# Gate and up weights of three expert groups moved as one whole expert per transfer, with each expert's columns dealt to four column groups of TensorE

## The reference, cut to what matters

```python
def expert_choice_moe(x, w_router, b_router, w_gate, w_up, w_down):
    cap = CAPACITY_FACTOR * s // N_EXPERTS                      # 2 * 256 // 16 = 32 tokens an expert
    aff = softmax(x @ w_router + b_router)                      # 16 experts
    gate, idx = lax.top_k(aff.transpose(0, 2, 1), cap)
    xs = x[bidx, idx]                                           # (16, 32, 1024)
    hid = silu(einsum('becd,edf->becf', xs, w_gate)) * einsum('becd,edf->becf', xs, w_up)
    ys = einsum('becf,efd->becd', hid, w_down) * gate[..., None]
    return zeros_like(x).at[bidx, idx].add(ys)
```

## Time and profile before

| What | Value |
|---|---|
| Time, median of 3 runs | 1989.81 us (1985.96 to 1994.66) |
| Profiled execution, its own time | 1984.02 us |
| Its span, first to last instruction | 1982.2 us |
| Mean granted TensorE clock | 0.970 |
| PE, DVE, ACT busy | 1744.1, 697.8, 298.5 us |
| Data moved | 599.64 MB, mean 303 GB/s |

### The profile page before, as it was taken

How to read it: one execution, slowest core, us unless ns; L and a number is a source line. 1 busy time by engine, 2 the same in 40 slices (tenths; PEclk the granted TensorE clock), 3 DMA queues, 4 the chain that set the end, 5 groups by cost and what they waited for, 6 DMA issues and landing times.

```text
span 1982.2 us, 20644 instructions
## 1 busy us (share of the span) xinstructions
PE 1744.1 (88%) x8516; PEld 904.6 (46%) x8516; DVE 697.8 (35%) x1456; ACT 298.5 (15%) x805; POOL 121.2 (6%) x105
## 2 busy tenths in 40 slices
PE   6999999999999999998878787777998878787776
PEld 3466988544679974474222122212474222122211
DVE  1673556977528986273010010101273010010101
ACT  1142000011611001252000010001253000010000
POOL 0000000000013510310000000000210000000000
PEclk9999999999999999999999899999999999999999
DMA  9890888755225643546999999999646999999997
GB/s 346 328 337 23 276 281 298 281 203 182 86 85 185 241 152 130 173 170 255 397 425 428 426 428 425 428 429 405 188 170 244 381 425 428 425 428 426 428 428 303
DMA packets 166925, 599.64 MB, mean 303 GB/s; under 512 B 18752, under 2 KB 77760, under 8 KB 135104
## 3 DMA queue, kind: packets, MB, share of 16 engines
q1 hardware_dynamic: 166606, 598.03, 76.9%
q10 hardware_dynamic: 242, 0.53, 0.1%
HBM read 594.75 MB, written 3.80 MB: 302 GB/s over the span
## 4 chain that ended last, share of the span: by engine, by line
PE 58%; DMA 35%; DVE 4%; ACT 1%; issue 1%; DVEq 0%; POOL 0%; SPq 0%; ACTq 0%; POOLq 0%
DMA extra<-in_w_down 13%; DMA extra<-in_w_up 12%; DMA extra<-in_w_gate 10%; PE ps L1195 9%; PE ps L1548 9%; PE ps L1308 6%; PE ps L1261 6%; PE ps L1233 5%; PE ps L1052 4%; PE ps L904 3%; PE ps L1446 3%; PE ps L1140 3%; PE ps L1018 1%; PE ps L795 1%; DVE extra L2234 1%
## 5 line engine op out<-in xcount | busy, mean ns | idle before, releaser
L1548 PE MATMUL ps<-ring,wide 128*32 128x512 f32 x2240 | 454.4, 619 | 91.0 <-DMA ring<-in_w_up 48.3
L1548 PEld LDWEIGHTS ps<-ring,wide 128*32 128x32 f32 x2240 | 116.1, 114 | 411.2 <-issue 292.2
L1548 PE MATMUL ps<-extra,wide 128*32 128x512 f32 x784 | 169.8, 720 | 77.0 <-DMA extra<-in_w_down 43.7
L3022 DVE TENSOR_TENSOR wide<-ps,wide 128x512 f32<-128x512 f32 x16 | 10.3, 686 | 520.6 <-PE ps L1548 520.6
L1195 PE MATMUL ps<-hT,ring 128*128 128x256 f32 (+1 forms) x1088 | 183.8, 331 | 0.0
L1195 PEld LDWEIGHTS ps<-hT,ring 128*128 128x128 f32 x1088 | 166.7, 191 | 17.2 <-issue 2.9
L1548 PEld LDWEIGHTS ps<-extra,wide 128*32 128x32 f32 x784 | 40.9, 128 | 204.7 <-issue 107.7
L1308 PE MATMUL ps<-ring,hT 128*128 128x512 f32 (+2 forms) x320 | 127.3, 555 | 0.3 <-issue 0.3
L2234 DVE SCALAR_TENSOR_TENSOR extra<-ring,sc,extra 128x512 f32<-128x512 f32 x140 | 109.8, 784 | 5.2
L3027 DVE COPY wide<-ps 128x512 f32<-128x512 f32 x8 | 5.5, 692 | 276.7 <-PE ps L1548 276.7
L1308 PEld LDWEIGHTS ps<-ring,hT 128*128 128x128 f32 x320 | 60.4, 190 | 62.0 <-issue 53.4
(11 more groups left out here) (362 smaller groups left out, 2022.1 us busy)
## 6 DMA issues: line engine op xcount, KB each, us to landing
ring<-in_w_gate SPq DMA_DIRECT2D x24, 4096.0 KB, 32.0
ring<-in_w_down SPq DMA_DIRECT2D x24, 4096.0 KB, 32.0
ring<-in_w_up SPq DMA_DIRECT2D x22, 4096.0 KB, 27.9
ring<-in_w_mod SPq DMA_DIRECT2D x24, 2048.0 KB, 13.8
ring<-in_w_up SPq DMA_DIRECT2D x44, 1024.0 KB, 8.0
extra<-in_w_gate SPq DMA_DIRECT2D x8, 4096.0 KB, 33.3
extra<-in_w_up SPq DMA_DIRECT2D x8, 4096.0 KB, 31.2
extra<-in_w_down SPq DMA_DIRECT2D x8, 4096.0 KB, 31.5
```

The source lines that it names most:

```text
L1548: last = mm(ps[bank + n][e * CAP:(e + 1) * CAP, :], lhs[:, k, e * CAP:(e + 1) * CAP], expert_at(n0, e, k, n * N), start=k == 0, stop=k == ...
```

## The change

The unit of gate and up in groups 2 to 4 becomes one whole expert, all eight k: one run of 32 KB for each partition. The bytes, the number of transfers, their order and their buffers stay. All gate and up units, those of group 1 too, are multiplied in a new way (`inner`): the 1024 columns of an expert are dealt in four quarters, columns c * 8 + 2j + h to quarter j (c from 0 to 127, h 0 or 1), and quarter j goes to column group j, whatever the expert. A matmul has 256 moving columns, read with a step of eight floats, in place of 512 contiguous ones. The hidden values lie in PSUM, `hid` and `hidT` in another order; the transposes read contiguously. The down part (`outer`) is multiplied as before. In the loop, `select` runs whole ahead of the first gate unit, since that unit now needs all eight k.

```diff
-        hidT = wide[:, 2048:3072].rearrange("p (k s) -> p k s", k=KD)
+        hidT = wide[:, 2048:3072].rearrange("p (e h j s) -> p e h j s", e=EG, h=2, j=4)
...
+        def unit_whole(n):
+            return n >= GROUP_UNITS and n % GROUP_UNITS < 2 * UNITS
+
         def unit_part(n):
             r = n % UNITS
+            if unit_whole(n):
+                return range(r, r + 1), range(KD)
             if unit_long(n):
...
+        def quarter(n, e, k, j):
+            return expert_row(n, e, k).rearrange("p (c j h) -> p j h c", j=4, h=2)[:, j, :, :]
...
-                            pe.wait_ge(*g_loaded(L, g, PAIR * q))
-                            if q < UNITS and ks[0] == 4:
-                                pe.wait_ge(*s.at("g_rows_by_act", 1))
-                            for k in ks:
-                                for n in range(2):
-                                    for e in es:
-                                        last = mm(ps[bank + n][e * CAP:(e + 1) * CAP, :],
-                                                  lhs[:, k, e * CAP:(e + 1) * CAP], expert_at(n0, e, k, n * N),
-                                                  start=k == 0, stop=k == KD - 1)
+                            pe.wait_ge(*g_loaded(L, g, PAIR * (part * UNITS + r)))
+                            for k in ks:
+                                if part == 0 and k == 4:
+                                    pe.wait_ge(*s.at("g_rows_by_act", 1))
+                                for e in es:
+                                    o = e % 2 * 2 * P
+                                    for j in range(4):
+                                        last = mm(ps[bank + e // 2][j * CAP:(j + 1) * CAP, o:o + 2 * P],
+                                                  xsT[:, k, e * CAP:(e + 1) * CAP], quarter(n0, e, k, j),
+                                                  start=k == 0 and e % 2 == 0,
+                                                  stop=k == KD - 1 and e % 2 == 1)
...
                     select(range(4)).then_inc(s.up("g_rows_done"), 1)
-                    select(range(4, 6))
-                    pe.wait_ge(*s.at("g_rows_by_dve", 1))
-                    experts(0, xsT, 0, range(1))
-                    select(range(6, 8)).then_inc(s.up("g_rows_done"), 1)
+                    if first:
+                        select(range(4, 6))
+                        pe.wait_ge(*s.at("g_rows_by_dve", 1))
+                        inner(0, range(1))
+                        select(range(6, 8)).then_inc(s.up("g_rows_done"), 1)
+                    else:
+                        select(range(4, 8)).then_inc(s.up("g_rows_done"), 1)
+                        pe.wait_ge(*s.at("g_rows_by_dve", 1))
+                        inner(0, range(1))
...
-                            k = 4 * hf + q
-                            last = nc.tensor.transpose(ps[4 + hf][:, q * P:(q + 1) * P],
-                                                       hid.rearrange("p (q k) -> p k q", k=KD)[:, k, :], ident)
+                            o = hf * N + q * P
+                            last = nc.tensor.transpose(ps[4 + hf][:, q * P:(q + 1) * P], hid[:, o:o + P], ident)
...
-                    av(hidT[:, 4:8, :], ps[5][:, :].rearrange("p (k s) -> p k s", k=4), ACT.Copy)\
+                    av(wide[:, 2560:3072], ps[5][:, :], ACT.Copy)\
...
-                    cp(hidT[:, 0:4, :], ps[4][:, :].rearrange("p (k s) -> p k s", k=4))\
+                    cp(wide[:, 2048:2560], ps[4][:, :])\
```

More of the change, by code:

```diff
@@ L463, in unit_part, with expert_row @@
             return range(EG), range(PAIR * r, PAIR * (r + 1))
-        def expert_at(n, e, k, o):
+        def expert_row(n, e, k):
             es, ks = unit_part(n)
@@ L468, in expert_at @@
             if pair_slot(n) == SLOTS + 1:
-                return once[i][:, q * EFF + o:q * EFF + o + N]
-            return pair_at(n)[:, (i * len(ks) + q) * EFF + o:(i * len(ks) + q) * EFF + o + N]
+                return once[i][:, q * EFF:(q + 1) * EFF]
+            return pair_at(n)[:, (i * len(ks) + q) * EFF:(i * len(ks) + q + 1) * EFF]
+        def quarter(n, e, k, j):
+            return expert_row(n, e, k).rearrange("p (c j h) -> p j h c", j=4, h=2)[:, j, :, :]
         def cc1(l, name, i=0, n=1):
@@ L1534, in select, with unit, inner, outer @@
                         return last
-                    def experts(part, lhs, bank, units=range(UNITS)):
+                    first = isinstance(g, int)
+                    def unit(q):
+                        return (g if first else 1) * GROUP_UNITS + q
+                    def inner(part, units=range(UNITS)):
+                        bank = 2 * part
                         for r in units:
-                            q = part * UNITS + r
-                            n0 = (g if isinstance(g, int) else 1) * GROUP_UNITS + q
+                            n0 = unit(part * UNITS + r)
                             es, ks = unit_part(n0)
-                            pe.wait_ge(*g_loaded(L, g, PAIR * q))
-                            if q < UNITS and ks[0] == 4:
-                                pe.wait_ge(*s.at("g_rows_by_act", 1))
+                            pe.wait_ge(*g_loaded(L, g, PAIR * (part * UNITS + r)))
[9 more added lines that the diff above has]
+                                                  stop=k == KD - 1 and e % 2 == 1)
+                            last.then_inc(tile_done, PAIR)
+                    def outer():
+                        for r in range(UNITS):
+                            n0 = unit(2 * UNITS + r)
+                            es, ks = unit_part(n0)
+                            pe.wait_ge(*g_loaded(L, g, PAIR * (2 * UNITS + r)))
                             for k in ks:
@@ L1547, in experts @@
                                     for e in es:
-                                        last = mm(ps[bank + n][e * CAP:(e + 1) * CAP, :],
-                                                  lhs[:, k, e * CAP:(e + 1) * CAP], expert_at(n0, e, k, n * N),
+                                        last = mm(ps[6 + n][e * CAP:(e + 1) * CAP, :], hidT[:, e, k % 2, k // 2, :],
+                                                  expert_row(n0, e, k)[:, n * N:(n + 1) * N],
                                                   start=k == 0, stop=k == KD - 1)
@@ L1563, in group @@
                     last.then_inc(s.up("g_weights_flipped"), 1)
-                    experts(0, xsT, 0, range(1, UNITS))
-                    experts(1, xsT, 2)
+                    inner(0, range(1, UNITS))
+                    inner(1)
                     pe.wait_ge(*s.at("g_hidden_ready", 2))
@@ L1575, in group @@
                     pe.wait_ge(*s.at("g_hidden_by_act", 1))
-                    experts(2, hidT, 6)
+                    outer()
                     pe.wait_ge(*s.at("g_result_by_act", 1))
```

## The result

| | before | after |
|---|---|---|
| Median of 12 runs | 1985.75 us (1982.50 to 1994.66) | 1992.95 us (1990.32 to 2001.78) |
| Profiled execution, its own time | 1984.02 us | 1997.1 us |
| Its span | 1982.2 us | 1995.3 us |

The ratio is 1.0043, with a 95% interval of 1.0028 to 1.0057: the change costs 7.2 us, where 3.3 us of gain were forecast. The two profiled executions differ by 13.1 us, and that is not the figure to explain: 4.4 us of it lie ahead of the experts (the last prefetched piece is issued at 939.82 where it was 935.46), in code that the change does not touch. Most executions of either kernel lie in a lower cluster and some about 10 us above it, with a few between, the changed kernel's profiled one among them; e3's profiled execution, of the upper cluster, has its delay ahead of the experts too.

The account below looks back on a forecast made before the run. The prediction took the 16 DMA engines to bound the expert groups; longer runs gave -3.3 us, all other terms 0, so 1989.8 - 3.3 = 1986.5 us for a median, range 1980 to 1999 us.

Parts of the forecast that it names:

- Which part binds: Expert stage: DMA engines set the pace from about a layer's sixth unit; TensorE counts in unit 0 and after the last landing.
- The strided moving read: Gate and up matmuls reading with a step of eight floats: taken at 0 us, unit 0 bounded by 3.64 and 14 us.
- the first rival: Strided reads at half pace: unit 0 takes 7.1 us, +7.0 us in all, 1993.5 us; chance 0.20 with smaller factors.
- The rule that was weighed against the trace: Moving read: a stream wants two hits on each 16-byte line, a step of four 32-bit floats still free; broken, first rival's result.
- Longer runs: 48 gate and up transfers: 32 KB packets save 0.069 us each, landing every 9.72 us, -3.3 us (bounds -6.6 and 0).
- The loop body: Loop group growing from 434 to 690 matmul records: code not fetched anew each pass, instruction code small, cost 0.
- cover argument: Loop body: if the longer code is fetched each pass, PE has 6 us of slack a unit to wait in.
- Clock: Gate and up batches of 3.6 to 7.2 us after idle time, lower mean clock than 0.95; cost 0, 1 us either way a layer.
- The start of a loop group: Whole `select` ahead of unit 0 adds 8 records, about 0.9 us, covered by the shorter unit and early-issued transfers; cost 0.
- Four streams in turn: Rival, every gate and up batch: strided streams served one after another, 14 us a unit, some 2270 us; chance 0.07.
- the runs stay short: Rival, gate and up transfers: packets stay 16 KB or their cost goes with bytes, 1989.8 us; chance 0.13.
- the prediction's own signs of error: Unit 0 over 5 us; gate and up batches following each other without a DMA wait; 32 KB packets making transfers slower.

Follow-up runs that it names:

- e3: Changed kernel with columns dealt in pairs of neighbouring floats, eight floats from pair to pair: 1985.65 us, ratio 1.0006 to the kernel before.
- e4: Changed kernel with group 1's gate and up units multiplied as before the change (512 contiguous columns): 1979.42 us, ratio 0.9965 to the kernel before.
- e5: Changed kernel with group 1 multiplied as before the change and groups 2 to 4 dealt in pairs of neighbouring floats: 1979.31 us, ratio 0.9969.
- e8: Kernel before, with output projection and expert down products reading moving columns at a step of eight floats (output wrong): 2066.00 us, single execution.
- e9: Kernel before, with output projection and expert down products reading moving columns at a step of four floats (output wrong): 2069.21 us, single execution.
- e10: Kernel before, with output projection and expert down products reading moving columns at a step of two floats (output wrong): 1997.44 us, single execution.
- e2: Changed kernel with columns dealt one by one, moving read stepping four floats instead of eight: 1991.83 us, ratio 1.0034 to the kernel before.
- e1: Changed kernel's matmuls with the transfers of before (runs of 16 KB): 1993.97 us, ratio 1.0043 to the kernel before.
- e6: Group 1 multiplied as before the change, rest as changed kernel, plus 128 unread one-column matmuls in each layer's group 1: 1984.83 us, ratio 0.9995.

## Why the prediction was wrong

- **Which part binds** was right. PE's batches in groups 2 to 4 took 7.56 us, where 3.6 were forecast, and e4, which keeps them, is with e5 the fastest kernel of the study: of the slow batches only unit 0 of each layer counted.
- **The strided moving read, taken at 0 us, is the step that failed.** It measured 3.92 us in unit 0, 7.8 us in both layers, and turned a gain into a loss. The evidence used was a stationary operand with the same step (0.111 us a step against 0.118), and that pace was read rightly; but e8 and e9 show that a moving stream behaves otherwise, 0.92 us against 0.43. The load of 191 ns in place of 140 in the earlier trace rows was no clear hint: in the kernel before, contiguous loads of other products show as much:

```profile
L1446 PEld LDWEIGHTS ps<-ring,hT 128*128 128x128 f32 x128 | 23.9, 190 | 28.8 <-issue 28.8
```

The price lay within the stated bounds (3.64 to 14 us), and the mechanism is that of the first rival, with 7.1 us a unit against 7.56. That the rival's 1993.5 us also meets the measured 1992.95 is luck. It starts from 1989.8, the median of three runs, and the median of twelve is 1985.75: its change was +3.7 us, the measured one +7.2. Missing in it are 0.9 us of the two units 0 and the 2.7 us of long steps.
- **The rule that was weighed against the trace** should have had more than the 0.20 given to that rival. e3 and e10 agree with the Trainium skill (SBUF — State Buffer, note on cachelines in the section on the DMA port swizzle; Advanced Engine Details and Errata, section Memory Cachelines) that two hits on each 16-byte line are wanted: 3.88 and 0.45 us with two, 7.56 and 0.92 with one. The step of four 32-bit floats that the Trainium skill (SBUF — State Buffer, the same note) calls free is not free for a moving operand: e2 has 7.43 to 7.58 us, e9 0.90.
- **Longer runs** were right in mechanism and size. The forecast was 9.72 us a transfer; measured are 9.71 to 9.72, so 3.5 us in all for the 3.3 forecast. e1 puts the runs of 16 KB back and lands every 9.79 us. The estimate by the Trainium skill (DMA: Bandwidth & Descriptors, section Why small descriptors are slow), 1.4 us, was too small: eight packets fewer on each engine save 0.075 us, 9 ns each.
- **The loop body, costed at nothing,** was wrong in a part that the prediction had not looked for. It is not fetched anew each pass, as was said, and PE never waited for it. But longer code is 62 packets in place of 54, and single ones of them, fetched inside the stream, fall together with a longer landing step: 2.7 us in the changed kernel, up to 3.2 in the others. e6 supports it, since it adds nothing but code that is off the path, and its two long steps come back. The prediction's cover argument asked whether the engine has time to wait, where it should have asked what the fetch takes from the engine that binds.
- **Clock** was right for fast units (e3: 3.9 to 6.6 us, 0.58), and did not arise in the changed kernel, whose slow batches kept the loop at 0.93 (0.95 before). Not foreseen was a lower clock ahead of unit 0, in the `select` of 4.54 us. The allowance of 1 us a layer for where the clock rises was needed: the last batch took 6.3 us or 5.3, over both layers 1.9 us less in e4 than before.
- **The start of a loop group** cost nothing, as forecast: `select` whole is 3.84 us, and unit 0 follows at once at 1040.05.
- **The other rivals.** Four streams in turn (14 us a unit) did not come: one stream alone has the same 0.92 us for 512 columns (e8) that four have. That the runs stay short did not come either.

Of the prediction's own signs of error the first held, unit 0 over 5 us. Its second did in group 1 of the layer: all eight gate and up units ran back to back for about 61 us (945.80 to 1006.46) without a wait for a transfer, and no cost beyond unit 0 is seen from it, since a batch of 7.4 us still gives buffers free faster than the queue fills them in 9.7.

## What to carry to other kernels

Before an operand is dealt out by a step, ask how many of its floats each 16 bytes give, and measure it on the operand that streams: the moving and the stationary side of a matmul are no evidence for each other. The same deal in pairs of neighbours costs almost nothing (3.88 against 3.66 us a unit), and a slow batch costs nothing either where its transfer is slower; so place the slow form in the loop, behind the transfers, and keep the fast one in the first batch, on which the queue waits (e4, e5: 6 us faster than the kernel before). Where the DMA queue binds, added instructions are added transfers, and single ones of them can cost time although the engine that runs them is hidden (e6).

## What the runs showed of the hardware beyond that

- A moving read of one 32-bit float from each 16 bytes runs at 0.47 times the contiguous pace at full clock (20.77 against 44.25 us for 48 records), with a step of 16 or 32 bytes alike, on one stream or on four.
- A 4 MiB transfer lands every 9.94 us in packets of 8 KB, 9.79 in 16 KB and 9.715 in 32 KB.
- Instructions come in packets of 16 KB, some 1.1 us each. Together with the 45th and the 61st of a kernel a landing step was mostly 0.8 to 1.6 us longer, with the others by at most 1.1 us or not visibly.
